# Last attention layer of a diffusion trunk on one Trainium2 core: another order of projections, tiles and tables

## The chip, the cores and the metric

The kernel runs on one core of one Trainium2 chip. The metric is the device time of one launch in microseconds (us). The whole network step is one program of five instruction streams: TensorE (PE, with its weight loads PEld), VectorE (DVE), ScalarE (ACT), GpSimd (POOL) and SyncE (SP, which issues most transfers). Streams meet only at semaphores.

## The reference

Four layers on 128 context tokens and 256 latent tokens (three tiles of 128 tokens, tile 0 the context). Layers 0 and 3 mix tokens by attention, layer 1 by pooling, layer 2 by retention; a mixture of experts (MoE) follows each. The attention, cut to what matters:

```
q, k, v = split(h @ w_qkv)                 # 8 query heads, 2 key heads, 2 value heads, 128 wide
q, k = rmsnorm(q) * q_norm, rmsnorm(k) * k_norm
context: softmax(q k^T / sqrt(128)) v over the context tokens; k and v (unrotated) are outputs
latent:  q, k rotated (axial rope); keys = [cached 128 keys, k], values = [cached values, v]
out = concat(heads) @ w_o ;  x = x + gate * out
```

## The kernel before, in words

The order of all work is written out by hand, once for each engine. In layer 3 the work runs as follows (function `pe_attention` for PE, `attention` in the DVE and ACT streams, the `l % 3 == 0` branch in the POOL stream).

- **Projections.** The weights `w_qkv` come as three panels of 512 columns: query heads 0 to 3, query heads 4 to 7, then two key and two value heads. Each panel is multiplied with the three token tiles, so nine projections of 8 matmuls each (16 instruction records each, since a float32 matmul leaves two), line L676. ACT copies each result from its PSUM bank into `qkv` (L2143) and counts `qkv_sb`.
- **Norm and rotation on DVE.** For the two query panels DVE squares and sums all three tiles (L1414, L1415), scales the means of 12 columns at once (L1420), waits for POOL to raise them to the power -0.5 (L2407), and then scales, multiplies by the gain and rotates each tile (L1430 to L1446). Keys go tile by tile, with one two-column power each (L2412). Tile 0 is not rotated. All of it waits first for the gain rows and the rotation table, which ACT's queue loads at the start of the layer (`attn_landed`). Counter: `qk_ready`.
- **Turning.** After the ninth projection PE transposes the eight query heads (three transposes each, L689, banks 4 to 6), ACT copies them to `qT` (L2160), which lies where `hT` was; then the two key heads with the cached keys (banks 0 and 1), copied to `kT` by three ACT instructions each.
- **Softmax loop.** For head h: `scores` (three matmuls, L751 to L753) into two banks; `maxima` on DVE (L1457, L1459); `soft` on ACT (three exponentials, L2178); `normalise` on DVE (L1463, L1465); `turn_probs` (seven transposes, L762); `probs_T` on ACT (two copies, L2187, L2189); `outputs` (seven matmuls, L776, L780); `output_T` on ACT (L2200). PE's order in the loop is scores(h+2), turn_probs(h+1), outputs(h). ACT's is soft(h+2), probs_T(h+1), output_T(h). DVE's is normalise(h+1), maxima(h+2).
- **After it** come six projections with `w_o` (L676, again two panels), the residual, the routing and nine MoE rows. SP loads a panel when the projections that used its slot are done.

Of the kernel before, what the change touches and what calls it, by code (L numbers as in the profile page):

```python
# [39 lines left out]
EPS = 1e-6  # L40
# [67 lines left out]
def build_trunk(nc, A, O, depth=DEPTH):  # L108
# [78 lines left out]
        start=mix0)  # L187
    (gqk, stat), _ = region(("qk_gain", [2, HD]), ("attn_stat", [96]), start=small_at)

    (prob, probT), dn_end = region(("prob", [2, 896]), ("probT", [2, 896]), start=dn2_at)  # L190
# [166 lines left out]
    def load_panel(sp, s, src_of, i=0, per=0):  # L357
# [3 lines left out]
        for n, (d, a) in enumerate(parts):  # L361
            sp.dma_start(d, a).then_inc(sem(f"panel_landed{s % 2}"), 48 - 16 * (len(parts) - 1) if n == 0 else 16)

    def panel_source(kind, l, i):
        a = l // 3
        if kind == "ada":
            if l < 3:
                return lambda d: [(d[:, KD // 2 * half:KD // 2 * (half + 1), :],
                                   A["ada_panels"][l, i, half].rearrange("p (k n) -> p k n", n=WIDE)) for half in range(2)]
            return lambda d: [(d[:, :, 0:ADA_N], ada_w[l, :, :, ds(i * ADA_N, ADA_N)])]  # L370
        if kind == "attn" and not isinstance(i, int) or kind == "attn" and i < 3:
            return lambda d: [(d[:, :, :], qkv_w[a, :, :, i * 512:(i + 1) * 512])]
# [443 lines left out]

    POOL_BANKS = (2, 3, 6, 5)

    def pe_pool_turn(pe, l, t):
# [396 lines left out]
    @block.tensor  # L1218
    def _(pe):
        pe.wait_ge(sem("const_landed"), 48)  # L1220
        for a in range(3):
            last = PE.transpose(ps[0][:, a * 96:(a + 1) * 96], vecs[0:96, a, :], ident[0:96, 0:96])
        last.then_inc(sem("vectors_ps"), 1)
        pe.wait_ge(sem("cond_ready"), 1)
        for t in range(TILES):
            pe_turn(pe, 0, t)
        pe_static_product(pe, 0)
        pe_static_product(pe, 1)
        pe_static_columns(pe, 0)
        passes = []  # L1230
        for l in range(depth):
            if l:
                if l > 1:
                    pe_keep_busy(pe, 6)
                if l % 3 != 1:
                    pe_turn(pe, 2 * l, 0)
                if l > 1:
                    pe_keep_busy(pe, 2)
            (pe_attention, pe_pool, pe_retention)[l % 3](pe, l)
# [14 lines left out]
        last.then_inc(sem("vectors_ps"), 1)  # L1254
# [9 lines left out]
    def _(dve):  # L1264
# [133 lines left out]
        def attention(l):  # L1398
# [72 lines left out]
            for h in range(HEADS):  # L1471
                if h + 1 < HEADS:
                    normalise(h + 1)
                if l == 0 and h == 6:
                    collect(3)
                if h + 2 < HEADS:
                    maxima(h + 2)

# [495 lines left out]
        for l in range(depth):  # L1974
            if l == 0:
# [6 lines left out]
            if l % 3 == 0:  # L1982
                attention(l)
            elif l % 3 == 2:
                retention(l)
            residual(l)
            if l == 0:
# [40 lines left out]
    def _(act_e):  # L2028
# [103 lines left out]
        def attention(l):  # L2132
# [61 lines left out]
            for h in range(HEADS):  # L2194
# [6 lines left out]
                if l == 0 and h == 5:  # L2201
                    stack_copy(3)

        def retention(l):
            e.dma_start(rnorm[:].rearrange("p h v -> p (h v)"), A["ret_norm"].broadcast_to([128, RH * RV])).then_inc(sem("table_landed"), 16)
            e.wait_ge(sem("decay_steps"), 1)
# [127 lines left out]
        for l in range(depth):  # L2334
# [4 lines left out]
            if l % 3 == 0:  # L2339
                attention(l)  # L2340
            elif l % 3 == 2:
# [21 lines left out]
    def _(pool):  # L2363
# [36 lines left out]
        for l in range(depth):  # L2400
            a = l // 3
            for t in range(TILES):
                inverse_root(2 * l, t)
            if l % 3 == 0:
# [62 lines left out]
```

## Time and profile before

| | us |
|---|---|
| median of three runs | 1507.73 |
| lowest, highest | 1502.98, 1510.9 |
| the profiled execution | 1509.87 |
| its span in the trace | 1508.1 |
| PE busy in the span | 1431.4 |
| DVE busy | 752.0 |
| ACT busy | 327.4 |
| mean granted clock of PE | 0.981 of full |

The span is 1.8 us shorter than the time of the execution that it was taken from. The last attention lies between 1179 us (first projection) and 1295 us (first projection with `w_o`) of the span. A granted clock of 1.00 is 2.4 GHz and one of 0.50 is 1.2 GHz.

### The profile page before, as it was taken

The page shows a single profiled execution, that of the slowest core. Times are in us where ns is not written, and L with a number is a line of the kernel's source. Part 1 is how long each engine was busy: PE and PEld are TensorE (multiplying, and loading weights), DVE is VectorE, ACT ScalarE, POOL GpSimd, SP SyncE. Part 2 cuts the span into 40 slices and gives each one's busy share as a digit, 9 for nine tenths or more (in the row PEclk, how much of TensorE's full clock was granted, in tenths as well). Part 3 has the DMA queues.
Part 4 walks back from the last instruction along what each step waited for, and adds up shares of the span by engine and source line. Part 5 has one row for each costly group of instructions (what it writes and reads, how often), then busy time and mean ns, then how long its engine had stood idle before and what let it go on. Part 6 is the DMA issues. An engine that isn't in the chain of part 4 may idle for free. (4 is left out here: it accounts for less than half of the span.)

```text
span 1508.1 us, 18194 instructions
## 1 busy us (share of the span) xinstructions
PE 1431.4 (95%) x6613; PEld 747.6 (50%) x6613; DVE 752.0 (50%) x1885; ACT 327.4 (22%) x729; POOL 92.6 (6%) x98
## 2 busy tenths in 40 slices
PE   6998998999899998999999999999999998999996
PEld 3335535444465443556666666445443446554442
DVE  1244304654536544666666666116545375155545
ACT  1105404111242110511111111023111305241112
POOL 0000011000220001000000000010001010110003
PEclk9999999999899999999999999999999998999998
DMA  9979967999888998745555554347998921038995
GB/s 380 405 307 374 420 245 315 365 424 422 336 348 353 422 423 327 267 130 171 174 179 181 181 180 168 139 171 313 424 422 336 377 94 63 24 145 354 423 422 210
DMA packets 124341, 430.27 MB, mean 285 GB/s; under 512 B 7424, under 2 KB 63584, under 8 KB 86752
## 3 DMA queue, kind: packets, MB, share of 16 engines
q1 hardware_dynamic: 108880, 390.64, 66.5%
q10 hardware_dynamic: 11920, 25.94, 4.5%
q0 software_dynamic: 3456, 12.58, 2.5%
q8 instruction: 50, 0.82, 0.2%
q14 instruction: 35, 0.29, 0.0%
HBM read 407.61 MB, written 21.53 MB: 285 GB/s over the span
## 5 line engine op out<-in xcount | busy, mean ns | idle before, releaser
L1072 PE MATMUL bank<-gate_up_weights,hT_gathered 128*64 128x512 f32 (+1 forms) x1280 | 253.7, 593 | 0.0
L903 PE MATMUL bank<-panel,hT 128*128 128x512 f32 x384 | 166.4, 593 | 1.8 <-ACT hT L2069 1.8
L1072 PEld LDWEIGHTS bank<-gate_up_weights,hT_gathered 128*64 128x64 f32 (+1 forms) x1280 | 81.1, 132 | 164.6 <-issue 164.6
L1086 PE MATMUL bank<-down_weights,actT 128*64 128x512 f32 (+1 forms) x640 | 138.5, 603 | 2.5 <-ACT actT L2296 2.5
L1521 DVE SCALAR_TENSOR_TENSOR ada_sums<-panel,cond_columns,ada_sums 128x384 f32<-128x384 f32 x224 | 121.2, 610 | 0.0
L903 PEld LDWEIGHTS bank<-panel,hT 128*128 128x128 f32 x384 | 72.8, 190 | 90.2 <-issue 88.7
L676 PE MATMUL bank<-panel,hT 128*128 128x512 f32 x240 | 105.1, 595 | 1.8 <-ACT hT L2069 1.8
L676 PE MATMUL bank<-panel,oT 128*128 128x512 f32 x192 | 84.3, 595 | 1.3 <-ACT oT L2200 1.3
L1374 DVE TENSOR_TENSOR residual_term<-bank,mixer_gate 128x512 f32<-128x512 f32 x24 | 16.5, 691 | 131.6 <-PE bank L676 71.0
L1057 PE MATMUL bank<-h_hi,P 128*128 128x512 f32 x192 | 81.6, 425 | 0.0
L2283 ACT ACTIVATE silu<-bank 128x256 f32<-128x256 f32 x36 | 13.8, 384 | 290.1 <-PE bank L1072 290.1
L1057 PE MATMUL bank<-h_lo,P 128*128 128x512 f32 x192 | 75.7, 394 | 0.0
L676 PEld LDWEIGHTS bank<-panel,hT 128*128 128x128 f32 x240 | 45.0, 190 | 60.9 <-issue 59.8
L1086 PEld LDWEIGHTS bank<-down_weights,actT 128*64 128x64 f32 (+1 forms) x640 | 34.8, 130 | 64.2 <-issue 55.7
L1848 DVE TENSOR_TENSOR y_rows<-bank,gate_of_slot 128x512 f32<-128x512 f32 x64 | 44.3, 691 | 40.0 <-PE bank L1086 38.0
L1821 DVE COPY h_gathered<-bank 128x512 f32<-128x512 f32 x36 | 24.9, 691 | 77.1 <-PE bank L1057 75.0
L676 PEld LDWEIGHTS bank<-panel,oT 128*128 128x128 f32 x192 | 35.8, 190 | 47.1 <-issue 47.1
L912 PE MATMUL bank<-panel,hT 128*128 128x256 f32 x256 | 57.3, 382 | 0.0
L1839 DVE TENSOR_TENSOR act<-bank,silu 128x256 f32<-128x256 f32 x32 | 13.6, 424 | 87.3 <-ACT silu L2283 87.3
L662 PE MATMUL bank<-panel,cond_columns 128*32 128x512 f32 x432 | 51.5, 599 | 2.7 <-DMA panel<-in_ada_panels 1.7
L912 PEld LDWEIGHTS bank<-panel,hT 128*128 128x128 f32 x256 | 48.1, 190 | 8.3 <-issue 2.1
L1057 PEld LDWEIGHTS bank<-h_hi,P 128*128 128x128 f32 x192 | 36.0, 188 | 31.5 <-issue 26.0
(355 smaller groups left out, 1975.6 us busy)
## 6 DMA issues: line engine op xcount, KB each, us to landing
gate_up_weights<-in_gate_up_halves SPq DMA_DIRECT2D x144, 1024.0 KB, 13.6
down_weights<-in_down_rows SPq DMA_DIRECT2D x72, 1024.0 KB, 13.7
panel<-in_ada_panels SPq DMA_DIRECT2D x54, 1024.0 KB
panel<-in_w_ada SPq DMA_DIRECT2D x16, 1536.0 KB
ada_panel_third<-in_ada_panels SPq DMA_DIRECT2D x18, 1024.0 KB
y_by_slot<-y_rows ACTq DMA_DIRECT2D x32, 512.0 KB, 8.2
panel<-in_ret_w_in SPq DMA_DIRECT2D x16, 1024.0 KB
panel<-in_attn_w_qkv SPq DMA_DIRECT2D x5, 2048.0 KB
```

The source lines that it names most:

```text
L662: last = PE.matmul(ps[7][32 * g:32 * g + 32, :], cond[:, 2 * g + kk, at:at + 32], src[:, 2 * g + kk, :], start=idx == lo and kk == 0, stop ...
L676: last = PE.matmul(ps[bank][:], lhs(k, t), panel[s % 2][:, k, :], start=k == 0, stop=k == nk - 1)
L903: last = PE.matmul(ps[t][:], hT[:, k, t * 128:(t + 1) * 128], panel[f % 2][:, k, :], start=k == 0, stop=k == KD - 1)
L912: last = PE.matmul(ps[3][:, t * 256:t * 256 + 256], hT[:, k, t * 128:(t + 1) * 128], panel[(f + 1) % 2][:, k, 0:256], start=k == 0, stop=k ...
L1057: last = PE.matmul(ps[half][:], Pm[:, j, t, :], part[:, t, half * 512:half * 512 + 512], start=t == 0 and n == 0, stop=t == TILES - 1 and ...
L1072: last = PE.matmul(ps[2][width * s:width * s + width, :], hg[:, j, k, width * s:width * s + width], gu_ring[w][:, 2 * k // KD, :, k % (KD ...
L1086: last = PE.matmul(ps[6 + half][width * s:width * s + width, :], actT[:, c, width * s:width * s + width], dn_ring[w][:, c, half * 512:half ...
L1374: V.tensor_tensor(tmp[:, m % 2, :], ps[3 * half + t][:], gate_bc[:, COND[t], half * 512:half * 512 + 512], ALU.mult).then_inc(sem("mix_ter ...
L1521: last = V.scalar_tensor_tensor(out, src, cond[:, k, 30 + o:31 + o], out, ALU.mult, ALU.add)
L1821: V.tensor_copy(hgt[:, 512:1024], ps[1][:]).then_inc(sem("row_hgt_dve"), 1)
L1848: V.tensor_tensor(ybuf[:, q % 2, o], ps[6 + half][:], grow[:, o], ALU.mult).then_inc(sem("row_y"), 1)
L2283: S.activation(silu[:], ps[2][:, 0:FE], ACT.Silu).then_inc(sem("row_silu"), 1)
```

## The change

Layer 0 is as before. Layer 3 gets functions of its own.

1. The panels come as queries 0 to 3, keys and values, queries 4 to 7 (`LATE_PARTS`). In the last panel the tiles are taken in the order 1, 2, 0 (`LATE_TILES`).
2. DVE and POOL go tile by tile for queries too: nine powers, of four, two and four columns. The squares share a buffer of 512 with the rotation.
3. After the eighth projection PE turns heads 0 to 3 and the keys, issues half of the ninth projection (bank 7), the scores of heads 0 and 1, the other half, and `turn_probs(0)`. Query heads 4 to 7 are turned inside the loop, through bank 7, one step before their scores. Turned heads 0 to 3 lie in the second half of `oT`, so `hT` stays whole for the ninth projection.
4. DVE does the squares of the last tile after normalise(1), then maxima(2), then its scaling, then normalise(2).
5. In ACT's loop probs_T(h+1) now stands ahead of soft(h+2), with a copy of a turned query head before or between them.
6. The rotation table and gains (`rope_late`, `gqk_late`) are issued on ACT's queue in layer 2, after `gate_shares`.

```
+    LATE_PARTS = (0, 2, 1)
+    LATE_HEADS = ((0, 4), (8, NQK), (4, 8))
+    LATE_BANKS = ((0, 2, 4), (5, 6, 3), (7, 3, 7))
+    LATE_TILES = ((0, 1, 2), (0, 1, 2), (1, 2, 0))
...
+            part = LATE_PARTS[i] if l else i
+            return lambda d: [(d[:, :, :], qkv_w[a, :, :, part * 512:(part + 1) * 512])]
...
+    late_qT = lambda h: oT[:, 4 + h, :] if h < 4 else qT[:, h, :]
...
+        panel_landed(pe, f + 2)
+        project(2, 0)
+        pe.wait_ge(sem("qkv_sb"), 9 * a + 6)
+        project(2, 1)
+        pe.wait_ge(sem("cache_landed"), 32 * (a + 1))
+        pe.wait_ge(sem("qk_ready"), 9 * a + 3)
+        for h in range(3):
+            turn_head(h, 4 + h)
+        pe.wait_ge(sem("qkT_sb"), spots[0])
+        turn_head(3, 4)
+        pe.wait_ge(sem("qk_ready"), 9 * a + 6)
+        for h in range(HEADS, NQK):
+            turn_head(h, h % 2)
+        pe.wait_ge(sem("qkv_sb"), 9 * a + 7)
+        project(2, 2, 0, KD // 2)
+        pe.wait_ge(sem("qkv_sb"), 9 * a + 8)
+        pe.wait_ge(sem("qkT_sb"), spots[NQK - 1])
+        scores(0)
+        scores(1)
+        project(2, 2, KD // 2, KD)
+        turn_probs(0)
+        for h in range(HEADS):
+            if 2 <= h <= 4:
+                pe.wait_ge(sem("qkT_sb"), spots[h + 2])
+                turn_head(h + 3, 7)
+            if h + 2 < HEADS:
+                scores(h + 2)
+            if h + 1 < HEADS:
+                turn_probs(h + 1)
+            if h == 1:
+                pe.wait_ge(sem("qkv_sb"), 9 * a + 9)
+                pe.wait_ge(sem("qk_ready"), 9 * a + 9)
+                turn_head(4, 7)
+            outputs(h)
...
+            for i in range(3):
+                for j in range(TILES if i < 2 else 2):
+                    squares(i, j)
+                    scale(i, j)
+                    if LATE_TILES[i][j]:
+                        rotate(i, j)
+            maxima(0)
+            maxima(1)
+            normalise(0)
+            normalise(1)
+            squares(2, 2)
+            maxima(2)
+            scale(2, 2)
+            normalise(2)
+            maxima(3)
+            for h in range(2, HEADS):
+                if h + 1 < HEADS:
+                    normalise(h + 1)
...
+            soft(0)
+            soft(1)
+            panel_rows(2, 2)
+            probs_T(0)
+            for h in range(HEADS):
+                if 2 <= h <= 4:
+                    queries(h + 3, h + 6, 7)
+                if h + 1 < HEADS:
+                    probs_T(h + 1)
+                if h == 1:
+                    queries(4, 7, 7)
+                if h + 2 < HEADS:
+                    soft(h + 2)
+                output_T(h)
...
+            if l == 2:
+                late_tables()
...
+                for i, (h0, h1) in enumerate(LATE_HEADS):
+                    for j, t in enumerate(LATE_TILES[i]):
+                        pool.wait_ge(sem("qk_ms"), 5 * a + 3 * i + j + 1)
+                        G.tensor_tensor(by_tile(64, h0, h1, t), by_tile(32, h0, h1, t), hpow[:, 0:h1 - h0], ALU.pow)\
```

## Rows read from the trace of the kernel before

Rows of the timeline are: start in the span (us), duration (us), engine, line, operation, output<-input, shapes, how many are merged, and in brackets the idle time before it with what ended it. Rows of the windows are: stretch (us), its length, busy us (and instructions) of PE, PEld, DVE, ACT and POOL, then the granted clock, the share of the DMA engines and GB/s.

**Rows 1.** Windows of the last attention, after its projections.
```profile
1244.00:1251.50 7.50, 4.60 (x34) 3.43 (x32) 3.59 (x12) 5.11 (x15) 0.70 (x1) 0.89 0.80 279
1251.50:1264.40 12.90, 10.33 (x30) 6.87 (x31) 5.25 (x18) 5.54 (x15) 0.00 (x0) 0.67 0.07 22
1264.40:1287.70 23.30, 22.28 (x153) 17.69 (x151) 13.34 (x43) 15.41 (x50) 0.00 (x0) 1.00 0.01 1
1287.70:1295.00 7.30, 4.39 (x36) 4.07 (x36) 1.12 (x4) 3.53 (x9) 0.00 (x0) 1.00 0.00 0
```

**Rows 2.** Timeline of PE: eight projections, turning, first scores, first turned probabilities.
```profile
1188.88 55.17 PE L676 MATMUL bank<-panel,hT 128*128 128x512 f32 x128 [0.87 <-ACT hT L2069]
1243.89 3.31 PE L689 MATMUL bank<-const_base,qkv 128*128 128x128 f32 x24
1249.21 0.55 PE L689 MATMUL bank<-const_base,qkv 128*128 128x128 f32 x3 [2.01 <-DVE qkv L1446]
...
1251.48 0.79 PE L751 MATMUL bank<-kT,qT 128*128 128x128 f32 x2 [0.81 <-ACT kT L2164]
...
1259.86 1.62 PE L762 MATMUL bank<-const_base,prob 128*128 128x128 f32 x7 [2.57 <-DVE prob L1465]
```

**Rows 3.** Timeline of PE: one turn of the loop, and its end.
```profile
1268.36 0.98 PE L762 MATMUL bank<-const_base,prob 128*128 128x128 f32 x7 [0.48 <-DVE prob L1465]
1269.18 0.39 PE L776 MATMUL bank<-probT,qkv 128*128 128x128 f32 x2
...
1270.74 0.39 PE L751 MATMUL bank<-kT,qT 128*128 128x128 f32 x2
...
1271.61 0.81 PE L753 MATMUL bank<-kT,qT 128*128 128x384 f32 x2
1272.49 0.98 PE L762 MATMUL bank<-const_base,prob 128*128 128x128 f32 x7
...
1289.27 0.99 PE L762 MATMUL bank<-const_base,prob 128*128 128x128 f32 x7 [1.59 <-DVE prob L1465]
...
1294.96 34.57 PE L676 MATMUL bank<-panel,oT 128*128 128x512 f32 x80 [0.67 <-ACT oT L2200]
```

**Rows 4.** Timeline of DVE: norm and rotation of queries 0 to 3, last key tile.
```profile
1204.02 0.69 DVE L1414 TENSOR_TENSOR qk_sq<-qkv 128x512 f32<-128x512 f32 x1 [14.64 <-DMA rope_tab<-in_k_rope]
...
1208.37 0.17 DVE L1420 TENSOR_SCALAR attn_stat<-attn_stat 128x12 f32<-128x12 f32 x1
1210.93 0.69 DVE L1430 TENSOR_TENSOR qkv<-qkv,attn_stat 128x512 f32<-128x512 f32 x1 [2.39 <-POOL attn_stat L2407]
...
1212.26 0.68 DVE L1430 TENSOR_TENSOR qkv<-qkv,attn_stat 128x512 f32<-128x512 f32 x1
...
1216.09 0.69 DVE L1430 TENSOR_TENSOR qkv<-qkv,attn_stat 128x512 f32<-128x512 f32 x1
...
1244.80 0.43 DVE L1414 TENSOR_TENSOR qk_sq<-qkv 128x256 f32<-128x256 f32 x1 [0.55 <-ACT qkv L2143]
```

**Rows 5.** Groups by line, POOL's powers (busy us, mean ns, idle before, releaser).
```profile
L2407 POOL TENSOR_TENSOR attn_stat<-attn_stat,const_base 128x12 f32<-128x12 f32 x2 | 4.6, 2276 | 38.1 <-DVE attn_stat L1420 38.1
L2412 POOL TENSOR_TENSOR attn_stat<-attn_stat,const_base 128x2 f32<-128x2 f32 x3 | 2.1, 698 | 16.4 <-DVE attn_stat L1426 16.4
```

**Rows 6.** Timelines of DVE and ACT: the softmax steps of one head.
```profile
1268.21 1.21 DVE L1457 TENSOR_REDUCE attn_stat<-bank 128x1 f32<-128x128 f32 x3
...
1269.66 0.37 ACT L2178 ACTIVATE prob<-bank,attn_stat 128x128 f32<-128x128 f32 x1 [1.31 <-DVE attn_stat L1459]
...
1271.28 0.18 DVE L1463 RECIPROCAL attn_stat<-attn_stat 128x3 f32<-128x3 f32 x1 [1.65 <-ACT prob L2178]
...
1271.61 0.51 ACT L2189 ACTIVATE probT<-bank 128x384 f32<-128x384 f32 x1
```

**Rows 7.** Layer 2, ACT's timeline at its first MoE row, and the window there.
```profile
1039.69 0.38 ACT L2283 ACTIVATE silu<-bank 128x256 f32<-128x256 f32 x1 [3.69 <-PE bank L1072]
...
1035.00:1040.00 5.00, 5.00 (x24) 1.68 (x21) 2.94 (x12) 1.30 (x2) 0.00 (x0) 1.00 0.54 180
```

More of the change, by code:

```diff
@@ L188, in build_trunk @@
     (gqk, stat), _ = region(("qk_gain", [2, HD]), ("attn_stat", [96]), start=small_at)
-    (prob, probT), dn_end = region(("prob", [2, 896]), ("probT", [2, 896]), start=dn2_at)
+    (rope_late, gqk_late), _ = region(("rope_tab_late", [2, 256]), ("qk_gain_late", [2, HD]), start=mix0 + 2 * size([TILES, D]))
+    (prob, probT, ropet_late), dn_end = region(("prob", [2, 896]), ("probT", [2, 896]), ("rope_t_late", [4 * HD]), start=dn2_at)
     assert dn_end <= dn2_at + 2 * size([2, D])
@@ L815, in pe_attention, with pe_late_attention, turn_head, project @@
             pe_static_columns(pe, 4)
+    late_qT = lambda h: oT[:, 4 + h, :] if h < 4 else qT[:, h, :]
+    def pe_late_attention(pe, l):
+        f, a = first_panel["mix", l], l // 3
+        turned = NQK * a
+        spots = {h: turned + i + 1 for i, h in enumerate((0, 1, 2, 3, 8, 9, 4, 5, 6, 7))}
+        def turn_head(h, bank):
+            b = ps[bank]
+            for t in range(TILES):
+                last = PE.transpose(b[:, t * 128:(t + 1) * 128], qkv[:, t, h * HD:(h + 1) * HD], ident)
+            if h >= HEADS:
+                last = PE.transpose(b[:, 384:512], ckv[:, 0, (h - HEADS) * HD:(h - HEADS + 1) * HD], ident)
+            last.then_inc(sem("qkT_ps"), 1)
+        def project(i, j, lo=0, hi=KD):
+            t = LATE_TILES[i][j]
+            for k in range(lo, hi):
+                last = PE.matmul(ps[LATE_BANKS[i][j]][:], hT[:, k, t * 128:(t + 1) * 128], panel[(f + i) % 2][:, k, :],
+                                 start=k == 0, stop=k == KD - 1)
+            if hi == KD:
+                last.then_inc(sem("proj_done"), 1)
+        def scores(h):
+            b0, g = 2 * (h % 2), h // (HEADS // KV)
+            if h >= 2:
+                pe.wait_ge(sem("prob"), 3 * (HEADS * a + h - 1))
+            if h >= 4:
+                pe.wait_ge(sem("qkT_sb"), spots[h])
+            PE.matmul(ps[b0][:, 0:128], late_qT(h)[:, 0:128], kT[:, g, 0:128], start=True, stop=True)
+            PE.matmul(ps[b0][:, 128:512], late_qT(h)[:, 128:256], kT[:, g, 128:512], start=True, stop=True)
+            PE.matmul(ps[b0 + 1][:, 0:384], late_qT(h)[:, 256:384], kT[:, g, 128:512], start=True, stop=True)\
+                .then_inc(sem("scores"), 1)
+        def turn_probs(h):
+            n = HEADS * a + h
+            pe.wait_ge(sem("prob_norm"), n + 1)
+            if h:
+                pe.wait_ge(sem("probT_sb"), 2 * n)
+            for c in range(7):
+                last = PE.transpose(ps[4 + c // 4][:, (c % 4) * 128:(c % 4) * 128 + 128],
+                                    prob[:, h % 2, c * 128:(c + 1) * 128], ident)
+                if c in (3, 6):
+                    last.then_inc(sem("probT_ps"), 1)
+        def outputs(h):
+            g = h // (HEADS // KV)
+            n = HEADS * a + h
+            pe.wait_ge(sem("probT_sb"), 2 * (n + 1))
+            if h:
+                pe.wait_ge(sem("oT_sb"), n)
+            v = lambda t: qkv[:, t, (NQK + g) * HD:(NQK + g + 1) * HD]
+            cv = ckv[:, 1, g * HD:(g + 1) * HD]
+            b = ps[6]
+            PE.matmul(b[:, 0:128], v(0), probT[:, h % 2, 0:128], start=True, stop=True)
+            for t in (1, 2):
+                for c, vals in enumerate((cv, v(1), v(2))):
+                    at = 128 + (t - 1) * 384 + c * 128
+                    last = PE.matmul(b[:, t * 128:(t + 1) * 128], vals, probT[:, h % 2, at:at + 128],
+                                     start=c == 0, stop=c == 2)
+            last.then_inc(sem("oT_ps"), 1)
+        panel_landed(pe, f)
+        pe_hT(pe, 2 * l, 0)
+        project(0, 0)
+        for t in (1, 2):
+            pe_turn(pe, 2 * l, t)
+        for t in (1, 2):
+            pe_hT(pe, 2 * l, t)
+            project(0, t)
+        panel_landed(pe, f + 1)
+        for t in range(TILES):
+            project(1, t)
+        panel_landed(pe, f + 2)
[32 more added lines that the diff above has]
+            outputs(h)
+        for i in range(3, 5):
+            panel_landed(pe, f + i)
+            if i == 3:
+                pe.wait_ge(sem("oT_sb"), HEADS * (a + 1))
+            for t in range(TILES):
+                if (i, t) == (4, 2):
+                    pe_turn(pe, 2 * l + 1, 0)
+                pe_project(pe, f + i, t, HEADS, lambda k, t: oT[:, k, t * 128:(t + 1) * 128], (0 if i == 3 else 3) + t)
@@ L1981, in _ @@
                 finish_mods(0, (0, 1), 2, KD // 2, KD)
-            if l % 3 == 0:
+            if l == 0:
                 attention(l)
-            elif l % 3 == 2:
+            elif l == 3:
+                late_attention(l)
+            elif l == 2:
                 retention(l)
@@ L2338, in _ @@
             norm(l, 0)
-            if l % 3 == 0:
+            if l == 0:
                 attention(l)
-            elif l % 3 == 2:
+            elif l == 3:
+                late_attention(l)
+            elif l == 2:
                 retention(l)
```

123 lines of the change are left out of this document (120 added, 3 removed).

## The prediction

> **What bounds the kernel now.** I read the page first: PE is busy nearly all the time, so only places where PE waits, or runs at the lower clock, can give anything. Then the windows over the last attention: after the projections PE is busy 4.60 of 7.50 us, then 10.33 of 12.90 us at a granted clock of 0.67, then 22.28 of 23.30 us at full clock, then 4.39 of 7.30 us [rows 1]. Then PE's timeline. During the projections PE never waits [rows 2]. Behind the ninth it waits 2.01 us for the rotated keys and 0.81 us for their copy; the first scores then run at 1.2 GHz; and it waits 2.57 us for the first probabilities, after which the clock is low again [rows 1, 2]. Why the first wait: the ninth result is in `qkv` 0.9 us after its last matmul was issued (1243.89 against 1244.80), and DVE needs until 1249.2 to square, scale and rotate that last key tile [rows 2, 4]. The eight query heads fill only 3.3 us of it.
>
> So the stretch to watch is from the start of the ninth projection to the start of the `w_o` projections. Eight projections took 1188.88 to 1243.89, 6.88 us each, so the ninth started at 1237.0 and the `w_o` projections at 1294.96 [rows 2, 3]: **58.0 us** before.
>
> **Prices.** From the rows: a projection 6.88 us. A turned query head 3.31 / 8 = 0.41 us; a key head has a fourth transpose, 0.55 us. turn_probs 0.82 us (1268.36 to 1269.18), outputs 1.56 us (1269.18 to 1270.74), scores 1.52 us (0.87 for the matmuls of 128 and 384 columns, 1270.74 to 1271.61, and three quarters of that, 0.65, for the last one of 384; its result comes 0.16 later, at 0.81) [rows 3]. The softmax chain of a head: maxima to first exponential 1.45 us (1268.21 to 1269.66), exponentials 1.62 us (to 1271.28), normalise until PE may turn 1.21 us (to 1272.49): 4.28 us [rows 3, 6].
>
> **The change, part by part.**
>
> *First four query heads and keys turned early.* PE turns them at 1237.0, right after the eighth projection: 4 x 0.41 + 2 x 0.55 = 2.75 us. Are they ready? Queries 0 to 3 by then have been through DVE for long. The last key tile is now the sixth projection, which ends around 1223.3; its work on DVE took 4.4 us before (1244.80 to 1249.2), so it is ready near 1228.5. The 2.01 us are gone. The copies to `kT` end near 1241, while PE does half a projection until 1243.2, so the 0.81 us are gone too. Nothing new is late here.
>
> *Is DVE in time?* A rotated tile of four heads costs 1.45 us of squares and sum (a third of 1204.02 to 1208.37), 0.17, the wait for POOL, and 3.83 us of scaling and rotation (1212.26 to 1216.09) [rows 4]. POOL's power was 2.28 us for 12 columns and 0.70 us for 2 [rows 5]. Four columns are not shown: bounds 0.70 and 2.28 us; on the line through both they cost 1.01 us, which I take, plus 0.11 us of handover (2.39 against 2.28). A tile is then 6.6 us, just under the 6.88 us of a projection. The eighth result is in `qkv` at 1237.9, so DVE is free at 1244.4, and scores(0) are there at 1243.2 + 1.52 + 0.16 = 1244.9. In time, by half a microsecond. It holds only because the tables land early: before, DVE started 14.64 us late for the rotation table [rows 4], which cost nothing then, because DVE had caught up by the last tile; with the new order it would.
>
> *Ninth projection as cover.* PE has, from 1237.0: turning 2.75, projection 6.88, two scores 3.04: 12.7 us, until 1249.7. Head 0's probabilities are ready at 1244.9 + 4.28 = 1249.2. The 2.57 us are gone. With them goes what brought the clock down, two waits of over 2 us. At low clock the two first scores took 5.8 us (1251.48 to 1257.29, the 2.57 us before 1259.86) against 3.04, and the second dip is of the same kind: together some 4.4 us [rows 1, 2].
>
> *Head 2.* PE goes on with turn_probs(0), scores(2), turn_probs(1), outputs(0), scores(3): 6.24 us, until 1255.9. DVE has normalise(1) until 1250.8, then the squares of the last tile, 1.6 us, and only at 1252.4 maxima(2). Add 4.28: 1256.7. A new wait of 0.8 us, the price of the squares ahead of the maxima. What is queued behind: everything in PE's loop.
>
> *The loop.* Head h+2's maxima cannot start before normalise(h+1) is done, which is when turn_probs(h+1) starts; so each head costs at least 4.28 us, as before, where it took 4.13 to 4.25. PE's own work is 3.90 us a turn, with a turned query head 4.31 us: the four heads moved into the loop lie mostly in the slack. In ACT's new order the exponentials stand behind two copies of turned probabilities. Those are ready 0.98 us after turn_probs began and are off ACT about 1.5 us after it; the exponentials could start at 1.45 us. So that costs near nothing, except for head 3, where the copy of query head 4 stands there as well (0.5 us). Two more times scores come out about 0.2 us late behind a turned head. Five intervals: 5 x 4.28 + 0.5 + 0.5 = 22.4 us; turn_probs(7) starts at 1279.1. From there to the `w_o` projections it is 5.69 us as before (1289.27 to 1294.96) [rows 3]: **1284.8**.
>
> *Panels and tables.* The second `w_o` panel is issued behind the ninth projection, now near 1249.7 instead of 1244; it is used 20 us after 1284.8. Hidden. The three table transfers now stand in ACT's queue in layer 2 behind `gate_shares`; ACT then waits 3.69 us for PE anyway, and the DMA engines are at 0.54 in that window for 180 GB/s, so 333 GB/s when full: 0.38 MB of tables (by their shapes) take 1.2 us of the 2.3 us that are free [rows 7]. I take 0; if weights are pushed back by it, 1.2 us is the upper bound.
>
> **Sum.** 1294.96 - 1284.8 = 10.2 us less. All behind it starts from PE's progress, also SP's loads, and shifts as a whole. The profiled execution of 1509.87 us becomes 1499.7; it lies 2.1 us above the median of 1507.73, on which I forecast **1497.5 us**. 0.5%, about what a measurement of this kernel can tell from no change, is 7.5 us. Bounds: without any wait in the new loop the gain would be 13.7 us (PE's work alone, and 1.5 us for the last copies); with the 12-column power price DVE is 1.7 us late and the gain is 8.4 us.
>
> **Weighed against the skill.** After the two waits over 2 us the granted clock fell to 0.50; with the waits of 0.5 to 1.6 us in the loop and at its end it stayed at 1.00 [rows 1 to 3]. The Trainium skill, "TensorE: Matmul & The Clock Gate", section "A second HAM failure mode: psum-queue depth-cycling", has a kernel whose short idles between groups of matmuls, cycling through PSUM banks, made the clock go up and down. By that rule the new loop, with its small waits, would dip and the gain would be near 7.4 us; by the rows it would not.
>
> **Rivals.**
>
> - *The clock dips once more in the loop.* One dip over two pairs of scores costs 5.8 - 3.04 = 2.8 us. Gain 7.4 us, 1500.3. For it: small waits are spread over more of the loop. Against: [rows 1], third and fourth. Chance 0.12.
> - *ACT becomes part of the chain.* If the exponentials wait 0.5 us for the copies in each of six heads, the chain is 4.8 us: gain 7.2 us, 1500.5. For it: ACT's copies end within 0.1 us of the moment when the exponentials could start. Chance 0.13.
> - *DVE late.* The tiles cost more than a projection, gain 8.4 us, 1499.3. Margin half a microsecond only. Chance 0.06.
> - *Other side: the clock stays low through the loop.* At 1.2 GHz PE's turn is twice 3.90, 7.8 us instead of 4.28, 3.5 us a head; from three heads on the gain is eaten, with six it is 21 us and the time 1518. Against: the same loop ran at 1.00. Chance 0.03.
> - *More than forecast*, above 12 us, if waits in the loop are smaller: 0.04.
> - *Forecast*, gain 8.5 to 12 us: 0.62.
>
> Faster by over 0.5% is the forecast, the larger gain and part of DVE late, less what the scatter of 1502.98 to 1510.9 can hide: 0.70; within 0.5% 0.27; slower 0.03. The range takes in the first three rivals and the bound of 13.7 us, with some scatter: 1492.5 to 1503.5 us.
>
> **What would show it.** Right: PE turns heads at once behind the eighth projection; no wait over 1 us up to turn_probs(2); granted clock 1.00 from the projections to `w_o`; a tile on DVE in 6.6 us; turn_probs every 4.3 to 4.8 us; `w_o` projections 47.8 us after the end of the eighth projection. Wrong: a clock of 0.50 between scores(0) and `w_o`, a power of four columns over 1.3 us, an interval of 4.8 us or more in every turn, or time lost in layer 2's first MoE rows.

## The result, and the profile after

| | before | after |
|---|---|---|
| median, us | 1507.53 (12 runs) | 1497.18 (12 runs) |
| lowest, highest | 1502.98, 1510.9 | 1494.29, 1504.27 |
| profiled execution | 1509.87 | 1498.89 |
| its span | 1508.1 | 1497.1 |
| mean granted clock in it | 0.981 | 0.982 |

The ratio is 0.9939, with a 95% interval of 0.9927 to 0.9951: faster by 0.6%, 9.2 us by the ratio and 10.4 us by the medians. The forecast was 1497.5 us.

The busy times hardly moved, so the gain is in waits and clock. From the page of the kernel after, PE's share of the span:

```profile
PE 1428.0 (95%) x6613; PEld 748.6 (50%) x6613; DVE 753.2 (50%) x1889; ACT 327.9 (22%) x729; POOL 94.3 (6%) x102
```

Windows of the kernel after, over the stretches that answer to [rows 1]: from the end of the eighth projection to `turn_probs(0)`, the loop up to `turn_probs(7)`, its end, and the `w_o` projections.

```profile
1232.90:1245.30 12.40, 12.31 (x49) 7.13 (x48) 9.84 (x25) 7.74 (x24) 1.01 (x1) 1.00 0.07 22
1245.30:1274.70 29.40, 26.40 (x182) 21.23 (x180) 18.54 (x57) 20.11 (x61) 1.01 (x1) 1.00 0.21 72
1274.70:1283.10 8.40, 7.04 (x35) 6.51 (x36) 0.00 (x0) 1.96 (x4) 0.00 (x0) 0.59 0.00 0
1283.10:1324.00 40.90, 40.90 (x102) 18.61 (x103) 6.24 (x16) 6.12 (x16) 7.43 (x7) 1.00 0.08 26
```

PE is busy for 12.31 of the first 12.40 us and the clock holds 1.00 there; in the loop it is busy 26.40 of 29.40 us. Only the third window, 8.40 us at a mean clock of 0.59, is worse than what stood there before. The timeline of PE in the same execution answers to [rows 2, 3]:

```profile
1184.78 48.30 PE L844 MATMUL bank<-panel,hT 128*128 128x512 f32 x112 [0.87 <-ACT hT L2282]
1232.92 2.11 PE L836 MATMUL bank<-const_base,qkv 128*128 128x128 f32 x15
...
1235.41 3.60 PE L844 MATMUL bank<-panel,hT 128*128 128x512 f32 x8
1238.85 0.38 PE L855 MATMUL bank<-kT,oT 128*128 128x128 f32 x2
...
1241.88 3.60 PE L844 MATMUL bank<-panel,hT 128*128 128x512 f32 x8
1245.31 0.93 PE L866 MATMUL bank<-const_base,prob 128*128 128x128 f32 x7
...
1247.59 0.93 PE L866 MATMUL bank<-const_base,prob 128*128 128x128 f32 x7
...
1252.08 0.98 PE L866 MATMUL bank<-const_base,prob 128*128 128x128 f32 x7 [0.48 <-DVE prob L1666]
...
1256.91 0.98 PE L866 MATMUL bank<-const_base,prob 128*128 128x128 f32 x7
...
1270.27 0.98 PE L866 MATMUL bank<-const_base,prob 128*128 128x128 f32 x7 [0.39 <-DVE prob L1666]
...
1274.72 0.98 PE L866 MATMUL bank<-const_base,prob 128*128 128x128 f32 x7 [1.91 <-DVE prob L1666]
...
1276.09 1.06 PE L884 MATMUL bank<-probT,qkv 128*128 128x128 f32 x4
...
1279.10 0.77 PE L880 MATMUL bank<-probT,qkv 128*128 128x128 f32 x2 [0.67 <-ACT oT L2467]
...
1283.10 34.57 PE L683 MATMUL bank<-panel,oT 128*128 128x512 f32 x80 [0.67 <-ACT oT L2467]
```

The three waits of [rows 2] (2.01, 0.81 and 2.57 us) have no successor: from the eighth projection's end at 1232.92 to `turn_probs(1)` no line carries a bracket. The row at 1276.09 is four records of `outputs(6)` in 1.06 us, which take 0.61 at full clock.

**Where the 11.0 us of this pair of executions lie.** The eighth projection's end to the `w_o` projections: 57.95 us before (1237.01 to 1294.96), 50.18 after (1232.92 to 1283.10): 7.8 us. The `w_o` projections start 11.86 us earlier in all, so 4.1 us were already there when the changed stretch began. They cannot be put down to the change: another execution of the same changed kernel reached this point at 1240.27, 7.4 us later (experiment 6). Part of it is the clock: from 600 to 640 us of the span it was granted 0.94 before, 1.00 after, and 0.91 in that other execution. Behind the attention 0.9 us is given back. The 24 transposes of the routed rows (L1031 before, L1157 after) fell into a stretch at low clock and took 4.49 us where the kernel before took 2.82; in the two other traces of the changed kernel they took 2.82 as well. PE's timeline after:

```profile
1333.60 4.49 PE L1157 MATMUL bank<-const_base,hT 128*128 128x128 f32 x24
```

So one pair of traces does not give the size of the change. The stretch does, read in several executions: 47.5 us without the low clock at its end, 50.2 with it (below).

### The profile page after: what moved, and what is told of

Read it like the earlier page. It is cut to its first block and busy times, and to the rows that moved or that the text cites. A ratio compares the mean times of both kernels' runs of the same rounds, so it can differ in the third digit from the quotient of the medians.

```text
span 1497.1 us, 18205 instructions
## 1 busy us (share of the span) xinstructions
PE 1428.0 (95%) x6613; PEld 748.6 (50%) x6613; DVE 753.2 (50%) x1889; ACT 327.9 (22%) x729; POOL 94.3 (6%) x102
## 5 line engine op out<-in xcount | busy, mean ns | idle before, releaser
L1029 PE MATMUL bank<-panel,hT 128*128 128x512 f32 x384 | 166.4, 592 | 1.8 <-ACT hT L2282 1.8
L1029 PEld LDWEIGHTS bank<-panel,hT 128*128 128x128 f32 x384 | 72.8, 190 | 90.2 <-issue 87.5
L844 PE MATMUL bank<-panel,hT 128*128 128x512 f32 x144 | 62.6, 593 | 1.8 <-ACT hT L2282 1.8
L1038 PEld LDWEIGHTS bank<-panel,hT 128*128 128x128 f32 x256 | 48.0, 190 | 8.3 <-issue 2.1
L1106 PE MATMUL bank<-panel,yT_even 128*128 128x512 f32 x96 | 49.2, 594 | 0.0
```

The lines of the kernel that those rows point to most:

```text
L844: last = PE.matmul(ps[LATE_BANKS[i][j]][:], hT[:, k, t * 128:(t + 1) * 128], panel[(f + i) % 2][:, k, :], start=k == 0, stop=k == KD - 1)
L1029: last = PE.matmul(ps[t][:], hT[:, k, t * 128:(t + 1) * 128], panel[f % 2][:, k, :], start=k == 0, stop=k == KD - 1)
L1038: last = PE.matmul(ps[3][:, t * 256:t * 256 + 256], hT[:, k, t * 128:(t + 1) * 128], panel[(f + 1) % 2][:, k, 0:256], start=k == 0, stop=k ...
L1106: last = PE.matmul(ps[3 * half + t][:], src[:, 4 * part + k // 2, t * 128:(t + 1) * 128], panel[s % 2][:, k, :], start=part == 0 and k == ...
```

## The experiments

In all of them "the stretch" runs from the end of the eighth projection to the first `w_o` projection. Ratios are against the kernel before on the same chip. The kernels `e1_busy_before` and `e10_busy_end` add matmuls on constants whose result nothing reads; none leaves work out.

**1. The kernel before, kept busy.** The claim: 4.4 us of the 10.2 are not waits but the low clock that follows them. `pe_keep_busy(pe, n)` issues n matmuls of 256 columns.

```
         pe.wait_ge(sem("qk_ready"), ...)      # three places in layer 3, before:
+        if l:
+            pe_keep_busy(pe, 4)               # the turned keys
...
+            pe_keep_busy(pe, 2)               # the first scores
...
+            pe_keep_busy(pe, 5)               # turn_probs(0)
```

> The kernel before, with small extra matmuls into an unused bank in layer 3 where PE waits: four before the turned keys, two before the first scores, five between scores(1) and turn_probs(0) (about 0.46 us each). Measure: the stretch from the end of the eighth projection to the first w_o projection, 58.0 us before. Theory (the clock fell because PE waited): the waits are filled, the granted clock stays 1.00 there, the first scores take 3.0 us instead of 5.8, and the stretch is 53.5 to 54.5 us; the time falls by about 4 us, ratio 0.997. Rival (the clock falls there whatever PE does between, for instance because transposes and small matmuls are too light a load): clock 0.50 stays and the stretch is 57.5 us or more; ratio 1.000.

Measured: 1503.33 us (1499.66 to 1505.0), ratio 0.9974 (0.9957 to 0.9991). The lines of its PE timeline that answer to [rows 2], and its window over the first scores:

```profile
1245.94 1.89 PE L603 MATMUL bank<-const_base 128*128 128x256 f32 x8
1248.11 0.55 PE L689 MATMUL bank<-const_base,qkv 128*128 128x128 f32 x3 [0.28 <-DVE qkv L1452]
...
1250.19 0.49 PE L755 MATMUL bank<-kT,qT 128*128 128x128 f32 x2
...
1256.36 0.98 PE L766 MATMUL bank<-const_base,prob 128*128 128x128 f32 x7 [0.72 <-DVE prob L1471]
...
1251.50:1264.40 12.90, 11.70 (x69) 8.97 (x68) 8.76 (x28) 7.36 (x24) 0.00 (x0) 1.00 0.01 4
```

PE still cannot go on before the keys and the first probabilities are there, but it is busy meanwhile; the clock stays at 1.00 where [rows 1] had 0.67, and the stretch is 53.9 us (1235.91 to 1289.79) instead of 58.0. Filling the waits with useless work gives 4.1 us. The other 6.4 us of the change (53.9 against the 47.5 of experiment 6) are a difference of two things. Up to `turn_probs(0)` 8.1 us went (20.45 us here, 12.38 there): the waits, and the turning of four query heads, which moved into the loop. From `turn_probs(2)` to `turn_probs(7)` 1.7 us came back (20.91 us here and in the kernel before, 22.64 after).

**2. The changed kernel without its cover.** The whole ninth projection is issued ahead of the turning, so nothing stands between scores(0) and `turn_probs(0)` but scores(1).

```
         project(2, 1)
+        pe.wait_ge(sem("qkv_sb"), 9 * a + 7)
+        project(2, 2)
         pe.wait_ge(sem("cache_landed"), 32 * (a + 1))
...
-        project(2, 2, 0, KD // 2)
...
-        project(2, 2, KD // 2, KD)
         turn_probs(0)
```

> The changed kernel, with the ninth projection done whole right behind the eighth, ahead of the turning; all else as changed. Theory (the ninth projection hides the first softmax chain): PE waits 4.28 - 1.52 = 2.8 us before turn_probs(0), the stretch grows from 50.2 to 53 us, and to 55 to 56 us if that wait brings the clock down as it did before; ratio to the kernel before 0.996 to 0.998. Rival (only the early keys matter): the wait is under 1 us and the stretch stays 50 to 51 us; ratio 0.994.

Measured: 1502.89 us (1498.92 to 1508.28), ratio 0.9973 (0.9956 to 0.999). PE's timeline, first scores and first `turn_probs`:

```profile
1251.07 0.46 PE L855 MATMUL bank<-kT,oT 128*128 128x128 f32 x2 [1.08 <-ACT kT L2442]
...
1257.21 1.75 PE L866 MATMUL bank<-const_base,prob 128*128 128x128 f32 x7 [2.87 <-DVE prob L1665]
```

Both waits are back, at nearly their old size (0.81 and 2.57 us), and `turn_probs` at 1257.21 takes 1.75 us instead of 0.98, so the low clock is back too, for a short time. The stretch is 53.3 us (1240.61 to 1293.90). The cover is worth 53.3 - 47.5 = 5.8 us of the 10.5 that the stretch gained: 4.2 us up to `turn_probs(0)`, and 1.6 us from there to `turn_probs(2)`, which is the low clock. The 53 us expected were counted from 50.2, a stretch with a low clock at its end that this trace does not have; what agrees is the growth, 4.8 to 5.8 us expected for the case that the clock falls. The other 4.7 us remain in this kernel; no run takes the early keys or the moved heads away by themselves. This division and that of experiment 1 overlap and must not be added.

**3. The tables late again.** The transfers of the rotation table and the gains are issued at the start of layer 3's attention.

```
+            late_tables()
             def panel_rows(i, j):
...
             gate_shares(l)
-            if l == 2:
-                late_tables()
```

> The changed kernel, with the gains and the rotation table loaded at the start of layer 3 as before. Theory (my step: it holds only because the tables land early): DVE starts 12 to 15 us later, wins back 2.5 us on each key tile and 0.3 us on each query tile, and is still 1.5 us late at maxima(0); PE waits 1 to 1.6 us at turn_probs(0), and the stretch grows by that. Rival (the key tiles give all of it back, as DVE caught up before): no wait at turn_probs(0), the stretch unchanged within 0.3 us. By time alone the two are not told apart.

Measured: 1502.16 us (1496.32 to 1508.87), ratio 0.9974 (0.9954 to 0.9994). PE's timeline, `turn_probs(0)` and `turn_probs(2)`:

```profile
1246.80 0.98 PE L866 MATMUL bank<-const_base,prob 128*128 128x128 f32 x7 [1.10 <-DVE prob L1666]
...
1253.93 0.33 PE L866 MATMUL bank<-const_base,prob 128*128 128x128 f32 x1 [0.79 <-DVE prob L1666]
```

DVE comes late by 1.1 us at `turn_probs(0)`, where there was no wait, and 0.3 us more at `turn_probs(2)` (0.79 against 0.48). The stretch is 49.1 us (1233.15 to 1282.25) at full clock against 47.5. The early tables are worth 1.6 us of this order; in the old order DVE's 14.64 us [rows 4] were worth nothing. The median lies 5 us above the changed kernel's, more than the 1.6 us in the trace; its runs spread over 12.6 us, so the median cannot be used for a difference of this size.

**4. The order on ACT.** The rival "ACT becomes part of the chain": the exponentials now stand behind the copies of turned probabilities. Here they go first again.

```
+                if h + 2 < HEADS:
+                    soft(h + 2)
                 if h + 1 < HEADS:
                     ...                       # probs_T(h+1), copies of turned queries
-                if h + 2 < HEADS:
-                    soft(h + 2)
                 output_T(h)
```

> The changed kernel, with ACT's loop in the old order: the exponentials of head h+2 ahead of the copies of head h+1's turned probabilities. Theory (the 4.45 us between two turn_probs in the changed trace, where the chain alone needs 4.28, are the exponentials standing behind the copies): intervals of 4.28 us, the one after turn_probs(2) 4.3 instead of 4.83, turn_probs(2) to turn_probs(7) 21.5 us instead of 22.64. Rival (PE's work with a turned head, 4.31 to 4.4 us, sets the interval): at most 0.3 us less in all.

Measured: 1497.11 us (1495.03 to 1497.36), ratio 0.9942 (0.9924 to 0.9961), the same as the change. First the changed kernel, DVE's maxima and ACT's steps of one head, to read against [rows 6]:

```profile
1261.34 1.22 DVE L1658 TENSOR_REDUCE attn_stat<-bank 128x1 f32<-128x128 f32 x3
...
1262.61 0.48 ACT L2463 ACTIVATE probT<-bank 128x384 f32<-128x384 f32 x1
1262.98 0.37 ACT L2452 ACTIVATE prob<-bank,attn_stat 128x128 f32<-128x128 f32 x1
```

From maxima to the first exponential it is 1.64 us; before it was 1.45 [rows 6]. ACT starts the exponentials where its second copy ends, not where the maxima are ready. With the order turned round it is 1.46 us again (1263.40 to 1264.86), and the loop's later intervals fall from 4.45 to a mean of 4.33 us. But PE's timeline of this kernel has a new wait, and its last one is shorter:

```profile
1257.13 0.55 PE L836 MATMUL bank<-const_base,qkv 128*128 128x128 f32 x3 [1.32 <-ACT qT L2436]
...
1276.36 0.98 PE L866 MATMUL bank<-const_base,prob 128*128 128x128 f32 x7 [1.59 <-DVE prob L1666]
```

Query head 5 is turned through the bank that the copy of query head 4 must first empty, and that copy now stands behind three exponentials. `turn_probs(2)` to `turn_probs(7)` takes 23.4 us (1252.94 to 1276.36) against 22.64 in the changed kernel, and the stretch 48.3 us against 47.5. Neither the 21.5 us expected nor the rival's "at most 0.3 us less" came true. Neither order is right for all heads: with the old order, the copies must still go first at h = 1, which `e6_best` below does; its interval there is 4.83 us, where it was 6.09 here.

**5. The squares.** My prediction put a wait before `turn_probs(2)` down to the squares of the last tile, which DVE does ahead of maxima(2).

```
             normalise(1)
-            squares(2, 2)
             maxima(2)
-            scale(2, 2)
+            squares(2, 2)
             normalise(2)
+            scale(2, 2)
```

> The changed kernel, with DVE's maxima(2) ahead of the squares of the last tile, and its scaling behind normalise(2). My step in the prediction gave the wait before turn_probs(2), 0.8 us forecast and 0.48 in the trace, as the price of the squares: by it the wait falls to 0.1 us or less. Rival (the chain from scores(2) sets it, the squares end before scores(2) do): turn_probs(2) still follows turn_probs(1) after 4.4 to 4.5 us, and the later scaling costs up to 0.5 us more before the turned head 4.

Measured (one run): 1503.14 us. DVE's timeline shows maxima(2) with nothing in front of it now:

```profile
1251.00 1.22 DVE L1658 TENSOR_REDUCE attn_stat<-bank 128x1 f32<-128x128 f32 x3 [1.45 <-PE bank L857]
```

It waits 1.45 us for scores(2). The wait before `turn_probs(2)` is 0.48 us in both kernels. DVE's timeline of the changed kernel says why:

```profile
1247.70 0.17 DVE L1618 TENSOR_SCALAR attn_stat<-attn_stat 128x4 f32<-128x4 f32 x1
1247.79 1.22 DVE L1658 TENSOR_REDUCE attn_stat<-bank 128x1 f32<-128x128 f32 x3
```

The squares end as scores(2) come out (the last of them start at 1246.94 and take 0.81 us: 1247.75). They cost nothing: maxima(2) starts 14.87 us after the eighth projection's end in the changed kernel and 14.86 here. What sets the wait is when PE gets to scores(2), behind half a projection and `turn_probs(0)`. That step of my prediction was wrong. The later scaling has a price, as the rival said. PE's timeline of this kernel, before the turned head 4:

```profile
1256.87 0.52 PE L836 MATMUL bank<-const_base,qkv 128*128 128x128 f32 x3 [0.60 <-DVE qkv L1627]
```

The changed kernel has no wait there. The stretch is 50.9 us (1236.14 to 1287.08), with the low clock at its end, against 50.2.

**6. The changed kernel again.** It ran twice more, since the low clock at the loop's end was not in the prediction.

> The changed kernel, as it is, profiled once more. Its first trace had the clock at 0.50 from turn_probs(7) to the w_o projections, 8.38 us instead of 5.69. Theory (where the clock falls at the end of the loop differs from one execution to the next): the stretch from the eighth projection's end to w_o is 47.5 us at full clock, or 50.2 us if it falls again. Rival (this order of work always brings it down): 50.2 us again, clock 0.50 after turn_probs(7).

> The changed kernel again, one look, for the same question as after_again: 47.5 us at full clock or 50.2 us with the low clock at the end of the loop.

Measured: 1500.01 us (1496.3 to 1501.9), ratio 0.9948 (0.9932 to 0.9965); and 1497.5 us for the single run. PE's timeline of the first, behind the eighth projection, `turn_probs(7)` and `w_o`, and the window between the last two:

```profile
1240.27 2.11 PE L836 MATMUL bank<-const_base,qkv 128*128 128x128 f32 x15
...
1282.06 0.98 PE L866 MATMUL bank<-const_base,prob 128*128 128x128 f32 x7 [1.91 <-DVE prob L1666]
...
1287.75 2.81 PE L683 MATMUL bank<-panel,oT 128*128 128x512 f32 x6 [0.67 <-ACT oT L2467]
...
1282.06:1287.75 5.69, 4.35 (x36) 4.02 (x36) 0.00 (x0) 1.96 (x4) 0.00 (x0) 1.00 0.00 0
```

The same waits, 1.91 and twice 0.67 us, and here the clock stays at 1.00: the end takes 5.69 us, as in [rows 3], and the stretch 47.5 us (1240.27 to 1287.75). In the single run it is 50.2 us again, at a clock of 0.50 from 1276 on. Over all seven traces whose loop ends in this way, the clock fell in three (the changed kernel's first trace, `after_third`, `e8_squares`) and held in four (`after_again` and experiments 2 to 4). In experiment 4 the wait before `turn_probs(7)` was only 1.59 us, as in the kernel before; of the six traces with 1.90 or 1.91 us it fell in three. In all three it fell about 1.2 us after `turn_probs(7)` had started, ahead of both waits of 0.67 us.

The time of an execution does not follow this end alone: the execution with the short stretch took 1501.9 us, the single run with the long one 1497.5, as the first had reached the stretch 7.2 us later.

**7. The end of the loop on PE.** The longest wait left is 1.91 us before `turn_probs(7)`. `outputs(6)` does not depend on it and can go ahead.

```
+            if h == HEADS - 2:
+                outputs(h)
             if h + 1 < HEADS:
                 turn_probs(h + 1)
...
-            outputs(h)
+            if h != HEADS - 2:
+                outputs(h)
```

On ACT, output_T(6) likewise goes ahead of probs_T(7).

> The changed kernel, with outputs(6) ahead of turn_probs(7) on PE, and output_T(6) ahead of probs_T(7) on ACT. Theory (PE waits 1.9 us for the last probabilities because no scores are left to do): outputs(6) fills 1.6 us of it, the wait before turn_probs(7) is 0.3 us, and from turn_probs(7) to w_o it is 3.8 us instead of 5.7: the stretch is 45.6 us at full clock, time about 2 us below the changed kernel. Rival (a wait for the copies of turned probabilities takes its place): outputs(7) starts 1.5 us after turn_probs(7), so only 1 us or less is won.

Measured: 1494.9 us (1494.33 to 1496.25), ratio 0.9926 (0.9911 to 0.994). PE's timeline, `outputs(6)`:

```profile
1274.23 0.46 PE L880 MATMUL bank<-probT,qkv 128*128 128x128 f32 x2 [1.18 <-ACT oT L2470]
```

Most of the wait did not go, it turned into one for the copy of outputs(5), which must leave the bank first. Behind `turn_probs(7)` comes the wait that the rival named, for the copies of the turned probabilities:

```profile
1277.59 0.49 PE L880 MATMUL bank<-probT,qkv 128*128 128x128 f32 x2 [0.80 <-ACT probT L2466]
```

The stretch is 46.9 us (1233.17 to 1280.09): 0.6 us less, not 1.9.

**8. Three more steps at the end.** `e6_best` adds half of the first `w_o` projection (heads 0 to 3) between `turn_probs(7)` and `outputs(7)`, and puts the exponentials first on ACT except at h = 1. `e7_bank` gives `outputs(6)` another bank, and lets the first half of the split projection wait for heads 0 to 3 only. `e9_last` lets the copies go first at h = 5 too.

```
e6:  +  if h == HEADS - 1:
     +      panel_landed(pe, f + 3)
     +      pe.wait_ge(sem("oT_sb"), HEADS * a + HEADS - 1)
     +      out_part(0, 4)                          # PE, ahead of outputs(7)
     +  if h != 1 and h + 2 < HEADS:  soft(h + 2)   # ACT, ahead of probs_T(h+1)
e7:  -  b = ps[6]
     +  b = ps[7 if h == HEADS - 2 else 6]          # and no wait for oT(5)
     +  pe.wait_ge(sem("oT_sb"), HEADS * a + 4)     # ahead of out_part(0, 4)
e9:  -  if h != 1 and h + 2 < HEADS:
     +  if h not in (1, 5) and h + 2 < HEADS:
```

> As e5_tail, and the first w_o projection is split around outputs(7): four of its matmuls between turn_probs(7) and outputs(7), three more while the last head's output is copied, the eighth after that; ACT's exponentials ahead of the copies again except in the step with query head 4's copy. Theory: PE waits for nothing from turn_probs(7) on; from the end of the eighth projection to the end of the six w_o projections it is 47.5 - 1.6 - 3.3 + 41.3 = 84 us (the changed kernel: 89.6 at full clock, 92.3 with the low clock in its trace); ratio to the kernel before 0.990 to 0.992. Rival (the loop before it sets the time, waits move to turn_probs(6) and (7)): 87 us or more, ratio 0.993 or above.

> As e6_best, with outputs(6) in bank 7, so that it need not wait until ACT has copied head 5's output out of bank 6. Theory (in e6_best PE waited 1.8 us before outputs(6) for that copy, which stood behind the last exponentials on ACT): the wait is gone, turn_probs(7) follows turn_probs(6) after 4.3 us instead of 6.0, and from the end of the eighth projection to the end of the w_o projections it is 85.7 us instead of 87.4 (the changed kernel: 89.6 at full clock); ratio to the kernel before about 0.990. Rival (the wait only moves on, to outputs(7) or to the split projection): 87 us or more.

> As e7_bank, with ACT's copies of head 6's turned probabilities ahead of the last exponentials, as the changed kernel has them. Theory (in e7_bank PE waited 1.3 us before outputs(6) for those copies): the wait is gone, turn_probs(7) follows turn_probs(6) after 4.45 us instead of 5.53, and from the end of the eighth projection to the end of the w_o projections it is 85.8 us instead of 86.8. Rival (the wait moves again): 86.5 us or more.

As the `w_o` projections now start inside the loop, the distance to their end counts. In the changed kernel it was 92.3 us (1232.92 to 1325.25), in `after_again` 89.6.

| | median (lowest to highest) | ratio (95%) | to the end of `w_o` |
|---|---|---|---|
| e6_best | 1494.32 (1491.86 to 1497.97) | 0.9918 (0.9901 to 0.9934) | 87.4 us |
| e7_bank | 1493.77 (1492.27 to 1499.4) | 0.9922 (0.9898 to 0.9946) | 86.8 us |
| e9_last | 1492.56 (1490.12 to 1494.82) | 0.991 (0.9896 to 0.9925) | 85.8 us |

Each step met the next wait. The distances expected were 84, 85.7 and 85.8 us: only the last was met, the first came out by its rival (87 us or more), and `e7_bank` between the two. With the bank free, `e7_bank` shows on PE's timeline that ACT's copy of head 6's turned probabilities stood behind the exponentials of head 7:

```profile
1274.22 0.49 PE L880 MATMUL bank<-probT,qkv 128*128 128x128 f32 x2 [1.31 <-ACT probT L2482]
```

With the copies first at h = 5 that goes too, and the loop's end in `e9_last` has one bracket left:

```profile
1271.02 0.98 PE L866 MATMUL bank<-const_base,prob 128*128 128x128 f32 x7
...
1275.47 0.98 PE L866 MATMUL bank<-const_base,prob 128*128 128x128 f32 x7 [0.34 <-DVE prob L1685]
1276.29 3.60 PE L890 MATMUL bank<-panel,oT 128*128 128x512 f32 x8
1279.72 0.38 PE L880 MATMUL bank<-probT,qkv 128*128 128x128 f32 x2
```

This kernel has the lowest median of the study. Its interval ends at 0.9925, below the change's, which begins at 0.9927. The intervals of `e5_tail` to `e9_last` overlap, so their order rests on the distances in one trace each, not on the times.

**9. The clock at the end.** The changed kernel with four matmuls on constants in the wait before `turn_probs(7)`.

```
+            if h == HEADS - 2:
+                pe_keep_busy(pe, 4)
             if h + 1 < HEADS:
                 turn_probs(h + 1)
```

> The changed kernel, with four small extra matmuls into bank 7 ahead of turn_probs(7), where PE waits 1.9 us. Theory (that wait is what brings the clock down in some executions): clock 1.00 through the end of the loop, 5.7 us from turn_probs(7) to w_o, and over the timed executions a median 0.5 to 1.5 us below the changed kernel. Rival (the waits of 0.67 us after it, or chance, bring it down): the low clock appears as often, the median is the same.

Measured: 1494.93 us (1493.28 to 1498.51), ratio 0.9929 (0.991 to 0.9947). PE's timeline:

```profile
1272.22 1.89 PE L610 MATMUL bank<-const_base 128*128 128x256 f32 x8
1274.28 0.98 PE L866 MATMUL bank<-const_base,prob 128*128 128x128 f32 x7 [0.17 <-DVE prob L1668]
...
1279.97 1.53 PE L683 MATMUL bank<-panel,oT 128*128 128x512 f32 x3 [0.67 <-ACT oT L2469]
```

The clock holds, the end takes 5.69 us, and the stretch is 47.5 us (1232.51 to 1279.97). As the clock holds in some executions without the filling as well, one trace cannot prove that the filling did it, and the times of the two kernels overlap. It stays open. One part of the rival is out: the waits of 0.67 us cannot be what brings the clock down, since in the changed kernel's first trace the row at 1276.09 is slow before the first of them, which ends at 1279.10.

## Why the prediction was right, and where it was not

**The sum.** Forecast: the stretch falls from 58.0 to 47.8 us. Measured: 47.5 us in `after_again` (57.95 - 47.48 = 10.5 us less), 50.2 us in the two traces of the changed kernel with the low clock at its end (7.8 us less). The measured ratio says 9.2 us, with an interval of 7.4 to 11.0 us that holds both, so the times cannot tell how often the low clock came. The stretch without it bears the sum out. That the median came within 0.3 us of the 1497.5 forecast is luck: in the traces, differences of several microseconds outside the stretch come and go with the execution.

**Keys early, the scores' wait, the cover: right.** No wait from the eighth projection to `turn_probs(1)`. Experiment 2 puts two of the three waits back by one edit.

**The clock, 4.4 us: right.** Experiment 1 gives 4.1 us with no other change.

**DVE in time by half a microsecond, and only with early tables: right.** The prices held: POOL took 1.01 us for four columns, and a tile 6.54 us where I had 6.6. POOL's and DVE's timelines in the changed kernel, the last tile before the first maxima:

```profile
1235.52 1.01 POOL L2706 TENSOR_TENSOR attn_stat<-attn_stat,const_base 128x4 f32<-128x4 f32 x1 [5.85 <-DVE attn_stat L1618]
...
1233.83 0.69 DVE L1616 TENSOR_TENSOR rope_t_late<-qkv 128x512 f32<-128x512 f32 x1 [0.32 <-ACT qkv L2432]
...
1236.57 0.69 DVE L1626 TENSOR_TENSOR qkv<-qkv,attn_stat 128x512 f32<-128x512 f32 x1 [1.12 <-POOL attn_stat L2706]
...
1239.68 0.69 DVE L1646 TENSOR_TENSOR qkv<-qkv,rope_t_late 128x512 f32<-128x512 f32 x1
1240.63 1.22 DVE L1658 TENSOR_REDUCE attn_stat<-bank 128x1 f32<-128x128 f32 x3 [0.27 <-PE bank L857]
```

The tile is done at 1240.37 and DVE then waits 0.27 us for scores(0): in time, with half the margin I gave it. Experiment 3 shows what the tables are worth, 1.6 us.

**The wait before `turn_probs(2)`: wrong cause.** I had 0.8 us "the price of the squares ahead of the maxima". It is 0.48 us, and the squares have no part in it (experiment 5). My own prices said so: scores(2) come out at 1249.7 + 0.82 + 1.52 + 0.16 = 1252.2, only 0.2 us before the 1252.4 at which I let DVE start.

**The chain of 4.28 us a head, and ACT's order "near nothing": too low.** The intervals from `turn_probs(2)` on are 4.83, 4.45, 4.46, 4.45 and 4.45 us, from 1252.08 to 1274.72. The exponentials start 1.64 us behind the maxima instead of 1.45, so the chain is 4.48 us (1261.34 to 1265.82) instead of 4.28; the rival "ACT becomes part of the chain" had the right mechanism, with 0.2 us a head where it had put 0.5. That a head costs "at least" its chain was not so either: the maxima can start up to 0.15 us ahead of `turn_probs`, and the kernel before ran at 4.13 to 4.25 us. On the other side, I had given two heads 0.2 us on top, which none of the intervals shows, and head 3 half a microsecond, which is 0.4. It made 22.64 us where I had 22.4. Two errors of opposite sign, so the total says nothing for its terms.

**The end of the loop: not foreseen.** I took 5.69 us "as before". In three of seven traces it was 8.4 us, among them two of the three of the changed kernel itself. A clock of 0.50 between scores(0) and `w_o` was one of my own signs of a wrong forecast; it came, behind a wait that the new order had made longer, 1.91 us before `turn_probs(7)` where it was 1.59 [rows 3]. The rival "the clock dips once more" had the mechanism and its size, 2.8 us, but put it over a pair of scores. Why it holds in some executions and falls in others, with the same waits in front, is open.

**The rule on short idles.** The Trainium skill, "TensorE: Matmul & The Clock Gate", section "A second HAM failure mode: psum-queue depth-cycling", says of another kernel that frequent short idles between groups of matmuls made the clock go up and down. In the loop the windows disagree: waits of 0.4 to 0.5 us at some turns, and 1.00 in every trace of the changed kernel. At the loop's end the clock did fall in three traces of seven, but behind one wait of 1.9 us, not behind frequent short ones. Experiment 2 has it again behind a wait of 2.87 us.

**Panels and tables: hidden,** as forecast. In the `w_o` projections PE is busy 40.90 of 40.90 us. In layer 2 ACT waits for PE as long as in [rows 7], 3.70 us against 3.69, so nothing shows that weights came later for the tables. ACT's timeline after:

```profile
1036.27 0.39 ACT L2576 ACTIVATE silu<-bank 128x256 f32<-128x256 f32 x1 [3.70 <-PE bank L1198]
```

## What to carry to other kernels

A wait of PE costs its own length, and here the waits of over 2 us cost a stretch at low clock behind them as well, those of 1.9 us in three executions of six, those of 1.8 us and less in none of the traces of this attention. The two costs can be told apart by filling the wait with matmuls whose result nobody reads, here 4.1 us of 10.5. Work that is ready and independent, cut in halves, is better filling: it covers the latency of another engine where it stands. After such a move every later step is as tight as its slack, so price the next engine in line (DVE had 0.3 us left, ACT none), and expect each wait removed at the end of a loop to show the next one: a bank to be emptied, then a copy behind other work. If a gain of 0.6% is to be measured by parts, read the changed stretch in several traces; medians over runs that spread by up to 12.6 us do not resolve a part of 1.6 us.

## What the hardware showed that was not expected

- The same program, with the same waits of 1.91, 0.67 and 0.67 us at the end of its last attention, ran them at a granted clock of 1.00 in one execution (5.69 us), and in another it fell to 0.50 about 1.2 us after the first of them (8.38 us).
- POOL's power with two inputs took 0.70 us for 2 columns, 1.01 for 4 and 2.28 for 12 [rows 5]: three points on one line, by my estimate 0.16 us a column over a base of 0.38.
- Two executions of the same changed kernel differed by 7.4 us ahead of the changed stretch, and in one window of 40 us there (600 to 640 us) the clock was granted 1.00 in one and 0.91 in the other.
